# A decoder step's gate matrix: built by one-hot products, or by adding single words to zeroed planes in memory

## The reference

```python
q = (tb @ wq).reshape(PEER_BLOCK, PEER_HEADS, 2, PEER_QHALF)
sc = jnp.einsum('thpd,hpnd->thpn', q, keys)
s1, i1 = lax.top_k(sc[:, :, 0], 16);  s2, i2 = lax.top_k(sc[:, :, 1], 16)
cand = s1[..., :, None] + s2[..., None, :]          # 256 a head, the best 16 are kept
eidx = i1 * 128 + i2 of the kept ones
g = jax.nn.softmax(top_s, axis=-1)
act = jax.nn.gelu(jnp.einsum('td,thkd->thk', tb, u_tab[eidx]))
return jnp.einsum('thk,thkd->td', g * act, v_tab[eidx])
```

## Time and profile before

| | us |
|---|---|
| three runs | 4112.72, 4115.00, 4124.71; median 4115.0 |
| the profiled execution, its own time | 4122.92 |
| its span in the profile | 4121.1 |
| PE busy in the span | 3593.3 (87%) |
| VectorE busy | 2679.8 (65%) |
| POOL busy | 1725.6 (42%) |
| ScalarE busy | 1038.0 (25%) |
| mean granted TensorE clock | 0.929 of full speed |

### The profile page before, as it was taken

One profiled execution on the slowest core, in us unless ns is written; L12 is line 12 of the kernel. 1 busy time (PEld: TensorE's weight loads), 2 busy tenths in 40 slices (PEclk: granted clock), 3 DMA queues, 4 the chain that ended last, 5 costly groups with the idle time before them and its releaser, 6 DMA issues.

```text
span 4121.1 us, 43667 instructions
## 1 busy us (share of the span) xinstructions
PE 3593.3 (87%) x13392; PEld 1910.1 (46%) x13392; DVE 2679.8 (65%) x5438; ACT 1038.0 (25%) x2269; POOL 1725.6 (42%) x1506
## 2 busy tenths in 40 slices
PE   6998987788888777765999999999999999996656
PEld 4665743444444344453444444444444444442222
DVE  2443743234343578885887778777877777777875
ACT  1323531443344267741111111111111111110111
POOL 0000100000000067743666667666666666666541
PEclk9999999887778799987999999999999999998778
DMA  3000113776777423237999999999999999999862
GB/s 129 31 23 19 47 61 110 233 215 205 213 220 213 143 85 123 106 140 263 403 391 374 372 387 382 374 377 381 384 384 372 374 391 383 373 370 345 324 244 83
DMA packets 398895, 1035.32 MB, mean 251 GB/s; under 512 B 37821, under 2 KB 131230, under 8 KB 396642
## 3 DMA queue, kind: packets, MB, share of 16 engines
q0 software_dynamic: 165888, 604.05, 38.1%
q1 hardware_dynamic: 208658, 373.22, 27.2%
q10 hardware_dynamic: 24144, 55.58, 3.7%
HBM read 983.59 MB, written 49.09 MB: 251 GB/s over the span
## 4 chain that ended last, share of the span: by engine, by line
PE 45%; DMA 4%; DVE 3%; issue 1%; POOL 1%; SPq 0%; ACT 0%; DVEq 0%
PE e_b L1913 21%; PE e_b L1940 21%; PE e_b L1899 3%; DMA wq<-in_p_prompt 1%; DMA out_y_prompt<-w_room 1%; DMA wq<-in_peer_u 1%; PE e_b L2125 1%; DVE facc L2045 1%; DMA wq<-in_ple_gate_b 1%; POOL u L1999 0%; POOL v L2007 0%; DVE u L2017 0%; DMA u<-in_peer_u,idx_all 0%; DVE ln_st L939 0%; DVE w_room L950 0%
## 5 line engine op out<-in xcount | busy, mean ns | idle before, releaser
L1940 PE MATMUL e_b<-w_room,e_room 128*128 128x512 f32 x2048 | 901.5, 593 | 7.4 <-DVE k_room L1953 7.4
L1913 PE MATMUL e_b<-wq 128*128 128x512 f32 x2048 | 903.5, 594 | 0.0
L1999 POOL DMA_INDIRECT u<-in_peer_u,idx_all x576 | 734.1, 1275 | 391.4 <-DVE act L2017 170.8
L2007 POOL DMA_INDIRECT v<-in_peer_v,idx_all x576 | 678.7, 1178 | 439.5 <-DVE facc L2045 172.6
L2017 DVE CUSTOM_DVE_ANT_0 u<-u,xb 128x1024 f32<-128x1024 f32 x576 | 704.8, 1224 | 188.3 <-DMA u<-in_peer_u,idx_all 178.8
L1649 POOL TENSOR_SCALAR u<-iota,e_room 128x128 f32<-128x128 f32 x256 | 279.2, 1098 | 840.7 <-ACT e_room L1631 741.8
L1940 PEld LDWEIGHTS e_b<-w_room,e_room 128*128 128x128 f32 x2048 | 389.8, 190 | 499.1 <-issue 489.8
L1913 PEld LDWEIGHTS e_b<-wq 128*128 128x128 f32 x2048 | 380.8, 191 | 431.2 <-issue 431.2
L2045 DVE SCALAR_TENSOR_TENSOR facc<-v,w,facc 128x1024 f32<-128x1024 f32 x317 | 406.9, 1284 | 2.3
L1906 ACT ACTIVATE wq<-e_b 128x512 f32<-128x512 f32 x256 | 139.4, 594 | 835.5 <-PE e_b L1899 701.3
L2045 DVE SCALAR_TENSOR_TENSOR wq<-v,w,wq 128x1024 f32<-128x1024 f32 x254 | 326.0, 1283 | 0.5
(11 more groups left out here) (337 smaller groups left out, 4127.9 us busy)
## 6 DMA issues: line engine op xcount, KB each, us to landing
wq<-in_peer_u SPq DMA_DIRECT2D x128, 512.0 KB
w_room<-in_peer_v SPq DMA_DIRECT2D x128, 512.0 KB, 4.1
w_room<-in_cache_k SPq DMA_DIRECT2D x172, 256.0 KB, 3.0
w_room<-in_cache_v SPq DMA_DIRECT2D x172, 256.0 KB, 3.0
gate_scratch<-v ACTq DMA_DIRECT2D x16, 2048.0 KB, 6.3
wq<-gate_scratch SPq DMA_DIRECT2D x32, 1024.0 KB
u<-in_cache_k SPq DMA_DIRECT2D x84, 256.0 KB, 3.0
u<-in_cache_v SPq DMA_DIRECT2D x84, 256.0 KB, 3.0
```

Source lines behind the costliest of these rows:

```text
L1913: last = pe.matmul(AQ[c % 2][:, 0:DT], UT[c % 2][:, k, :], x1Td[:, k, :], start=(k == 0), stop=(k == KC - 1))
L1940: last = pe.matmul(OQ[i % 2][b][:], WT[n % 2][:, c, m * P:m * P + P], Vd[(4 * n + c) % NVD][:, b * 512:b * 512 + 512], start=(c == 0), sto ...
L1999: pool.indirect_dma_start(u[x % NU], None, a["peer_u"], bass.IndirectOffsetOnAxis(ap=idx_all[:, t, h, j:j + 1], axis=0)).then_inc(s_u[x % ...
L2007: pool.indirect_dma_start(v[y % NV], None, a["peer_v"], bass.IndirectOffsetOnAxis(ap=idx_all[:, t, h, j:j + 1], axis=0)).then_inc(s_v[y % ...
```

## The change

The gate matrix is no longer made by products. It has a plane in HBM for each of the four dense tiles, 16384 experts by 128 rows, 8.4 MB each. In `prompt_attention` SP fills all four with zeros, 32 stores of 1 MB from a zeroed tile. In the first block of `peer`, when the dense batch of a head is ranked, `rank_gate_dve` also makes the word address of each choice (`slot_of` = expert * 128 + row), and POOL issues, for each of the head's 16 choices and each plane, one indirect DMA that adds 128 single words, the gates, at 128 addresses. In one plane each such DMA waits until the one before it has landed; the four planes are independent. `load_g` waits for all of them and reads each plane by itself, 2 KB in one piece instead of 512 B.

The order of the batches changes: batch e is head e // 2, dense when e is even, gathering when it is odd, so each of the eight sequences has a dense and a gathering batch of one head. All projections (`Q_AT`) are dealt out over slots 12 to 240, one matmul a slot and three in slots 16 to 19 of a sequence, none in every eighth; the ranking steps are dealt out by a table of costs in us (`COST`), up to about 2.9 a slot and none in slots 16 and 17. All eight x1 tiles are transposed in slots 0 to 7 and the keys in 8 to 11; the loads for them are set between the first groups of pages. The two sample batches of 64 rows become one of 128. Worked through, the tables give: the first dense batch is ranked in slots 24 to 34, the last dense one (e = 14) in 225 to 235 after its scores, the last gathering one in 244 to 254, the sample batch in 279 to 289; SLOTS is 291 and was 438.

```diff
-        gate_d = nc.dram_tensor("gate_scratch", (NDT * P // GB * PK, PK * GB), F32, kind="Internal").ap()
+        gate_d = [nc.dram_tensor(f"gate_scratch{n}", (PK * PK, P), F32, kind="Internal").ap() for n in range(NDT)]
+        s_gz = sem("s_gz")
...
                 ahead(sp)
+                sp.wait_ge(s["zero"], 2)
+                for g in gate_d:
+                    flat = g.rearrange("(p e) t -> p (e t)", p=P)
+                    for n in range(0, PK * P, 2 * D):
+                        sp.dma_start(flat[:, n:n + 2 * D], zeros[:]).then_inc(s_gz, 16)
...
                 pool.memset(qz[:], 0.0).then_inc(s["zero"], 1)
-                pool.wait_ge(s["zero"], 1)
+                pool.memset(zeros[:], 0.0).then_inc(s["zero"], 1)
+                pool.wait_ge(s["zero"], 2)
...
+            if e < NBAT and group == 0:
                 ch.sync()
-                ch.add(dve.scalar_tensor_tensor(out=ids, in0=i12[0:R, 0], scalar=float(PK), in1=i12[0:R, 1],
-                                                op0=ALU.mult, op1=ALU.add))
+                ch.add(dve.tensor_scalar(slot_of[:, :, h, :], idf[:], float(P), pcol[:], ALU.mult, ALU.add))
...
-        SEQ_SLOTS, RS = 32, 16
+        SEQ_SLOTS = 32
         MIXED = DB * SEQ_SLOTS
-        NQUAD = DT // 4
-        Q_AT = {**{12 + n: (n,) for n in range(4)}, **{16 + n: range(4 + 3 * n, 7 + 3 * n) for n in range(4)}}
...
+        while step < NBAT * 2 * KC:
+            c = x % SEQ_SLOTS
+            n = 3 if 16 <= c < 20 else 0 if c % 8 == 7 else 1
...
+        COST = {"top": 1.6, "pairs": 2.0, "best": 1.5, "place": 1.7, "index": 3.7, "gate": 1.4}
...
-        def quad_pool(pool, q):
...
+        def scatter_pool(pool, h):
+
+            pool.wait_ge(s["tk"], 2 * h + 1)
+            if h == 0:
+                pool.wait_ge(s_gz, 16 * NDT * PK * P // (2 * D))
+            for j in range(TOPK):
+                for m in range(NDT):
+                    wait(pool, s_gs[m], 16 * (h * TOPK + j))
+                    pool.indirect_dma_start(gate_d[m].rearrange("e (t o) -> (e t) o", o=1),
+                                            bass.IndirectOffsetOnAxis(ap=slot_of[:, m, h, j:j + 1], axis=0),
+                                            gd[:, m, h, j:j + 1], None, compute_op=ALU.add).then_inc(s_gs[m], 16)
...
-            src = gate_d.rearrange("(b p) (c t) -> p b c t", p=PK, t=GB)[:, :, 4 * n:4 * n + 4, :]
-            sp.dma_start(G[n % 2], src).then_inc(s_g[n % 2], 16)
+            for m in range(NDT):
+                if n == 0:
+                    sp.wait_ge(s_gs[m], 16 * PH * TOPK)
+                src = gate_d[m].rearrange("(p c) t -> p c t", c=PK)[:, 4 * n:4 * n + 4, :]
+                sp.dma_start(G[n % 2][:, m, :, :], src).then_inc(s_g[n % 2], 16)
...
-                for q in range(NQUAD):
-                    quad_pool(pool, q)
+                pool.iota(pcol[:], pattern=[[0, 1]], base=0, channel_multiplier=1,
+                          allow_small_or_imprecise_dtypes=True).then_inc(s["zero"], 1)
+                for h in range(PH):
+                    scatter_pool(pool, h)
```

More of the change, by code:

```diff
@@ L170, in program @@
             s_wo = sem1("s_wo")
+            zeros = sb1("zeros", [P, 2 * D])
             def load_w_out(sp):
@@ L1153, in peer @@
         UT = [room([P, KC, P]) for n in range(2)]
-        G = [room([P, NB, 4, GB]) for n in range(2)]
+        G = [room([P, NDT, 4, P]) for n in range(2)]
         gA = [room([P, DT]) for n in range(2)]
@@ L1255, in sample_q_pe @@
             for k in range(KC):
-                last = pe.matmul(B[b][:, at:at + SR], ring[e % NR][:, k, m * P:m * P + P], x1S[:, k, :],
+                last = pe.matmul(B[b][:, at:at + SR], ring[w % NR][:, k, m * P:m * P + P], x1S[:, k, :],
                                  start=(k == 0), stop=(k == KC - 1))
@@ L1552, in peer @@
-        Q_AT = {**{12 + n: (n,) for n in range(4)}, **{16 + n: range(4 + 3 * n, 7 + 3 * n) for n in range(4)}}
-        def ranked_at(e):
-            if e < PH:
-                return SEQ_SLOTS * e + 26, 2 if e < PH - 1 else 1
-            return MIXED + RS * (e - PH) + 19, 1
-        def rank_steps(e):
-            at, pace = ranked_at(e)
-            steps = {at + pace * n: ("top", n) for n in range(2 * UN)}
-            at += 2 * UN * pace
-            for n, step in enumerate((("pairs", 0), ("best", 0), ("best", 1), ("best", 2), ("best", 3), ("place", 0))):
-                steps[at + n] = step
-            at += 6 if pace == 1 else 10
-            steps.update({at: ("index", 0), at + 1: ("index", 1), at + 3: ("gate", 0)})
-            return steps, at
@@ new lines, in peer @@
+        S_Q = S_TURN + 1
+        S_SCORE = S_Q + 9
+        Q_AT, Q_DONE = {}, {}
+        x, step = Q_FIRST, 0
+        while step < NBAT * 2 * KC:
+            c = x % SEQ_SLOTS
+            n = 3 if 16 <= c < 20 else 0 if c % 8 == 7 else 1
+            for _ in range(min(n, NBAT * 2 * KC - step)):
+                e, y = step // (2 * KC), step % (2 * KC)
+                Q_AT.setdefault(x, []).append((e, y))
+                if y % KC == KC - 1:
+                    Q_DONE[e, y // KC] = x
+                step += 1
+            x += 1
@@ new lines, in peer @@
+        Q_OUT, SCORE_AT, SCORED_AT, RANK, EXP_AT = {}, {}, {}, {}, {}
+        for (e, m), x in Q_DONE.items():
+            Q_OUT[x + 1] = (e, m)
+        for e in range(NBAT + 1):
+            for r in range(2):
+                x = Q_DONE[e, 1] + 2 + 2 * r if e < NBAT else S_SCORE + r
+                SCORE_AT[x], SCORED_AT[x + 1] = (e, r), (e, r)
+        COST = {"top": 1.6, "pairs": 2.0, "best": 1.5, "place": 1.7, "index": 3.7, "gate": 1.4}
+        slot, used = 0, 0.0
+        for e in range(NBAT + 1):
+            ready = Q_DONE[e, 1] + 4 if e < NBAT else S_SCORE + 2
+            steps = [("top", n) for n in range(2 * UN)] + [("pairs", 0)] + [("best", n) for n in range(UN)] + [
+                ("place", 0), ("index", 0), ("index", 1), ("gate", 0)]
+            for name, n in steps:
+                first_slot = ready + (2 if name == "top" and n >= 4 else 0)
+                if slot < first_slot:
+                    slot, used = first_slot, 0.0
+                while used >= 2.5 or (slot < MIXED and slot % SEQ_SLOTS in (16, 17)):
+                    slot, used = slot + 1, max(0.0, used - 2.9)
+                RANK.setdefault(slot, []).append((e, name, n))
+                used += COST[name]
+                if (name, n) == ("index", 0):
+                    EXP_AT.setdefault(slot, []).append(e)
@@ L2326, in _ @@
                 load_x(sp, 1)
-                for h in range(HS):
-                    sp.dma_start(idx_all[SR:P, NGT, h, :], idx_all[0:SR, NGT, HS + h, :]).then_inc(s["half"], 16)
-                    sp.dma_start(gt_all[SR:P, NGT, h, :], gt_all[0:SR, NGT, HS + h, :]).then_inc(s["half"], 16)
                 for x in range(NCH):
```

413 lines of the change are left out of this document (147 added, 266 removed), and 3 rows, old and new, of the table names.

## The result

| | before | after |
|---|---|---|
| median of four runs beside each other, us | 4114.3 (4112.7 to 4124.7) | 4010.7 (4008.1 to 4014.2) |
| profiled execution, its own time and span, us | 4122.9, 4121.1 | 4008.1, 4006.0 |
| first gather of experts issued, us | 1883.9 | 1776.0 |
| POOL busy, us | 1725.6 | 2232.5 |
| VectorE busy, us | 2679.8 | 2576.0 |

The changed kernel takes 0.974 of the time of the one before (95% interval 0.973 to 0.976), 104 us less. The prediction said 3840, that is 275 less. The sign is right, but the gain is well under half of the forecast and the time is 171 us longer than the 3840.

What follows compares the result with a forecast made beforehand. Stages behind barriers bound the kernel; only the first expert gather moves, from 1883.9 to 1603 us. 281 gained and 2 lost from 4122.9 give 3844, less 8 for the median 3836, say 3840; range 3745 to 4150.

Steps and rivals of the forecast that it cites:

- The view of what bounds it: Whole kernel: a row of stages behind barriers; later stages keep their length, only their start at 1883.9 us moves.
- The block's own work: First block apart from the scatter: attention ends near 1429 us, all its work near 1550 (1480 to 1660).
- The tail: First block after the attention, from folding heads to the last rank batch: 121 us, sample projections 35 of them.
- The zero fill: Zeroing 33.5 MB of planes from 410 us: done near 525, costs nothing; at half rate up to 40 us.
- The rounds: Scatter on POOL, four adds a round: 6.2 us (5.0 to 7.2), 128 rounds 794 us, ending about 1603.
- rival 3: Scatter adds dear on POOL, yet paying: round 7.2 to 8.3 us, time 3964 to 4104 us; chance 0.15.
- Own work ends last: First block: rounds of 5.0 to 5.7 us, POOL done near 1460, before the tail; 3713 to 3783 us; chance 0.15.
- DMA contention: Attention: scattered words at 86 ns each slow page loads, stretching it some 90 us; time 3873 us; chance 0.10.
- The chain decides: Scatter: dependent adds in a plane take over 8.4 us a round, so slower; 4322 us at 10; chance 0.17.
- It doesn't do what it says: Attention: ranks pile up, VectorE falls behind, attention grows by what the second half loses; about 4115 us; chance 0.02.
- Neighbours on SBUF: POOL issue: GpSimd shares its SBUF interface with VectorE's two-input instructions; gathers 0.94 against 1.94 us agree; sum doesn't need it.

Runs made afterwards that it cites:

- half and quarter runs: Kernel after, with each of the 512 adds cut from 128 words to 64 (half) or 32 (quarter): 3954.9 us and 3901.9 us, one run each.

## Why the prediction was right in sign and wrong in size

**The view of what bounds it: right.** Both long stages kept their length; from the first gather on it is 4006.0 - 1776.0 = 2230 us against 2237. All that moved is when they begin, as the prediction's sum was built.

**The block's own work: right within 11 us.** The first dense batch was forecast for 806, the first add came at 809.4. A sequence was forecast at 84.6 + 6 = 90.6 and took (1374.9 - 758.2) / 7 = 88.1. The attention was to end at 1429 and ends at 1421. The clock is the likely reason that the cost was nearer to the lower bound: with full-width projections between the value matmuls it is mostly at its upper level. The value slots of sequences 3 and 5, and of the last one, in which no projection is left:

```profile
1039.00:1072.00 33.00, 28.35 (x156) 14.26 (x149) 30.46 (x133) 6.02 (x21) 26.63 (x17) 0.90 0.92 234
1213.00:1242.00 29.00, 24.86 (x146) 11.45 (x138) 27.13 (x120) 5.54 (x20) 24.34 (x16) 0.96 0.88 211
...
1390.00:1422.00 32.00, 28.13 (x120) 13.87 (x112) 23.06 (x90) 3.85 (x10) 26.61 (x18) 0.50 0.82 190
```

They answer to the value slots in the earlier trace rows, where the clock was 0.50. Over the eight sequences the value slots stood at 0.50 to 0.69 before; after, the first seven, with 16 to 18 records of the projections in each, stand at 0.82 to 1.00 and the eighth, with none, at 0.50. The levels are 1.2 GHz (0.50) and 2.4 GHz (1.00); a value between them is a stretch that has both. The link to the projections rests on this comparison; what holds the clock up was not tried apart.

**The tail: one more term mis-sized.** Forecast 121 us; measured 1560.7 - 1421.1 = 139.6. The sample projections were sized at 35 us, from a range of 25 to 48, and took 54.85, outside it; the other terms together were forecast at 86 and took 85:

```profile
1419.18 1.93 PE L1543 MATMUL e_b<-w_room 128*32 128x512 f32 x8 [0.43 <-ACT w_room L1530]
...
1448.41 15.31 PE L966 MATMUL e_b<-w_room,mixS 128*64 128x512 f32 x32 [13.54 <-DMA w_room<-in_w_out]
...
1472.46 54.85 PE L1276 MATMUL e_b<-w_room,wq 128*128 128x64 f32 x256 [0.56 <-ACT w_room L1733]
```

Here the prediction carried a price over from a row at another clock. Its 0.275 us a record was measured at the upper level. In the kernel after, the same matmuls, now with no other matmuls between them (257 matmul records in the stretch against 419), run at the lower one. The stretch before, the stretch after, and the line itself after:

```profile
1764.00:1813.00 49.00, 47.36 (x419) 46.73 (x419) 38.86 (x136) 34.46 (x87) 35.82 (x33) 1.00 0.65 216
...
1472.00:1528.00 56.00, 54.85 (x257) 54.69 (x257) 0.36 (x1) 1.19 (x2) 46.39 (x31) 0.50 0.53 99
...
L1276 PE MATMUL e_b<-w_room,wq x256: 421/421/446, 1472.5 to 1526.9; 128*128 128x64 f32 x128
```

In the kernel after, the longer sample projections cost nothing, being under the scatter's overhang; in the kernel without a scatter they count in full.

**The zero fill: right.** The kernel after shows the 32 stores of 1 MB at 27.0 us from issue to landing, in a stretch with a DMA share of 0.59 and 242 GB/s instead of 0.09 and 33. The last of them was in place at 508.0, forecast was near 525, and the mix behind it begins at 574.0 against 572.8.

```profile
gate_scratch<-zeros SPq DMA_DIRECT2D x32, 1024.0 KB, 27.0
```

**The rounds: this is the step that failed.** The prediction bounded a round by 4 x (0.95 + 0.30) = 5.0 and 4 x (1.5 + 0.30) = 7.2 and took 6.2, "the middle and the measured mean of the nearest row". Measured is 4 x (1.547 + 0.30) = 7.4, with the few long ones 7.5: the term lies above even its upper bound. It is 1.3 us more in each of 128 rounds, 165 us, nearly all of the 171. The start 3 us later and 5 us more between the last add and the gather are the rest of the shift of the gather, 1776.0 against 1603; the 7 us that the later stages were shorter go the other way.

Two readings went wrong there. First, the middle had no row behind it: the 1.262 of the earlier trace rows is a mean over gathers of 0.94 and of 1.94, not the price of a dearer instruction, and says nothing of an add. Second, the upper bound's 1.5 came near the measured 1.547, but not for its reason, so that was luck. It argued that reading, adding and writing make half as many descriptors again. The queue shows 4.5 times as many packets as for a plain write (144 against 32), and the half and quarter runs show that the surcharge is mostly on the instruction and not on its words.

The time came out in rival 3 of the prediction (round 7.2 to 8.3, 3964 to 4104), which had been given 0.15 against 0.41.

**The other rivals.** *Own work ends last* (0.15) is what happens with plain writes, in 3788.6 us against the 3713 to 3783 that the rival named: a round at the price of a gather was right for a write without the add. *DMA contention* (0.10) took 86 ns a word from the direct queue. From the row of the adds' queue above, 0.168 x 1076 x 16 / 73728 = 39 ns a packet, of which there are 144 an add; and the attention was not longer for it. *The chain decides* (0.17) fell with 4.4 us a link, against the 8.4 us a round that it needed. *It doesn't do what it says* (0.02) fell with the last ranking at 1560.5, where the block's own work was forecast to end near 1550.

**Neighbours on SBUF.** The prediction weighed a rule of the Trainium skill's page "GPSIMD Engine Reference", section 1, Specifications, that GpSimd shares its SBUF interface with VectorE's two-input instructions. It can't be the cause of the add's price: in the row 1560 to 1775 VectorE is idle, and the adds take 1.54 to 1.56 us there, with the same median, 1.547, as beside it. For the gathers the trace of the kernel before agrees with the page: of the 272 gathers that had a VectorE instruction of over 1 us beside them for less than a tenth of their time, none took over 1.2 us; of the 509 that had one for nine tenths or more, 46% took over 1.5.

**What stays open.** What GpSimd does in the 0.59 us is not in the trace. Why the clock stays at 0.50 in the sample projections wasn't tried. One instruction with several indices for each partition, which would spread the fixed part, was not tried; nor was starting the next block's gathers between the adds.

## What to carry to other kernels

The price of an instruction that no row shows has no measured middle: carry both ends through the sum, and don't average a neighbour's contention into it. Where it is issued 512 times in a row, 0.3 us decides the result. A duration read from a row holds at the granted clock of that row; look whether the work beside it stays. Before taking an operation that reads and writes memory for free elsewhere, ask whether the engine that issues it pays by the instruction: if so, use fewer and wider ones, or do the arithmetic on an engine with room and write plainly. When a change leaves one engine alone in a stretch (here 215 us of POOL), a run without that work gives the floor, and the gap to it is all that a cheaper way of doing that work can gain.

## What the runs showed of the hardware

- An indirect write of 4-byte words takes POOL 0.895 us for 64 and 0.958 for 128 words; with an add it takes 1.320, 1.411 and 1.547 for 32, 64 and 128. Between two stand 0.30 us. By these steps about four fifths of an add of 128 words would be paid whatever their number, an estimate.
- An add has 144, 80 and 48 packets in the DMA queue for 128, 64 and 32 words; a plain write has 32 for 128 and for 64.
- An indirect add of 128 words to HBM lands 4.2 us (2.9 to 8.4) after its issue, beside page loads at a DMA share of about 0.7.
- The 73728 packets of the adds take 39 ns each of a DMA engine; they raised the share of the attention from 0.67 to 0.82 without making it longer.
- The granted clock in the value slots was between 0.50 and 0.69 before, between 0.82 and 1.00 with projections between the narrow matmuls, and 0.50 in the one sequence that had none left.
- The 256 matmul records of the sample projections took 0.275 us each at a granted clock of 1.00 and 0.421 at 0.50.
